# Two row tiles' latent queries and keys turned by VectorE blocks and transfers, in another order of work

## The chip, the cores and the metric

The kernel runs on one core of a Trainium2 chip. The metric is the device time of one execution in microseconds. The kernel before takes 1025.74 us, the median of three runs (1025.30 to 1026.27).

## The reference

Two transformer blocks run one after the other on 256 rows (the sequence) of 1024 features in fp32: a first block (short convolution, gated feed-forward, sliding-window attention, feed-forward) and a second block, of which the middle concerns us. It projects the normalised rows with `w_in` into a latent part (256 + 128 + 32 features), the queries and keys of a retention layer (512 each), its values and its gates (512 each). The latent part is normalised and expanded by `w_uq` and `w_ukv` into 8 heads of queries, keys (64 plain + 32 rotated features) and values; softmax attention over all 256 rows follows. Retention (8 heads of 64) and the latent attention together go through `w_o`. Two feed-forward networks stand before and behind.

```python
def mla_group(c_q, c_kv, k_pe_raw, pos_f, q_norm, w_uq, kv_norm, w_ukv):
    q = (rms_norm(c_q, q_norm) @ w_uq).reshape(B, S, H, 64 + 32)
    q_nope, q_pe = q[..., :64], rope(q[..., 64:], pos_f)
    kv = (rms_norm(c_kv, kv_norm) @ w_ukv).reshape(B, S, H, 64 + 64)
    k_nope, v = kv[..., :64], kv[..., 64:]
    k_pe = rope(k_pe_raw[:, :, None, :], pos_f)[:, :, 0]
    ...
    s = einsum('bqhd,bkhd->bhqk', qn, k_nope) + einsum('bqhr,bkr->bhqk', qp, k_pe)
    p = softmax(s * MLA_SCALE, axis=-1)
    return einsum('bhqk,bkhd->bqhd', p, v)

def second_block(x, ...):
    h = x + 0.5 * swiglu_2(rms_norm(x, ffn1_norm), ...)
    proj = rms_norm(h, mix_norm) @ w_in
    c_q, c_kv, k_pe, r_q, r_k, r_v, r_g = split(proj, [256, 384, 416, 928, 1440, 1952])
    a = mla_group(c_q, c_kv, k_pe, ...)
    r = retention_group(r_q, r_k, r_v, r_g, ...)
    h = h + concatenate([a, r], axis=-1) @ w_o
    h = h + 0.5 * swiglu_2(rms_norm(h, ffn2_norm), ...)
    return rms_norm(h, final_norm)
```

## The kernel before

The 256 rows are two row tiles (t = 0 and 1) of 128. All weights stream from HBM in chunks of 128 x 1024 fp32 (512 KB), in one order fixed by tables of chunk numbers (`C_X`, `C_U`, `C_WO`) and, on the host side, by `weight_chunks`. SyncE loads chunk n into one of four raw buffers once chunk n - 4 has been split (`load_behind`). ScalarE makes `w_high` of a raw chunk, and VectorE `w_low`, the rest; twelve split chunks have room (`RING`), and chunk n + 12 may be split when TensorE has used chunk n for both row tiles. A product of one row tile with a chunk is three passes of two matmuls each: high by high, low rows by high, high by low weights. The first product with a chunk (t = 0) waits for its `w_high` before the first pass and for its `w_low` before the third (`chunk_passes` with `split`).

The order of work is written out by hand. `walk_latent` calls `step(name, ...)` in one sequence, every engine walks the same sequence, and each carries out in order the steps that it has a function for; semaphores tie them together. So an engine's own instructions keep the order of that list. The names of the stage:

- `X(i, t, c)`: chunk c of projection i for row tile t (i = 0 latent, 1 and 2 the retention queries and keys, 3 values, 4 gates). ScalarE copies each finished projection from PSUM (`copied`); the next one of that row tile waits for this copy (`x_out`).
- `R` (`refill`), `high`, `low`: the split of one more chunk on ScalarE and VectorE, and on SyncE the load four chunks further.
- `LAT(t)`: the latent rows are normalised and turned by three TensorE transposes. `U(t)`: the expanding product with three chunks (18 matmuls), whose results ScalarE copies as `mq` (queries), `mk` (keys), `mv` (values), and VectorE's rotation of the 32 position features of `mq`. `KPE(t)`: the rotation of the shared key part, copied into `mk`.
- `MT(t)`: 16 TensorE transposes of 128x96 turn `mq` and `mk` by heads into PSUM; ScalarE copies the queries to `mqT`, VectorE the keys to `mkT`.
- `MS(v)`: round v = 0 to 7 computes the scores of two heads (two matmuls). `MS(v)` waits from v = 2 for the exponentials of round v - 2 (`mp_ready`), whose bank it overwrites. VectorE takes the maxima, `ME(v)` the exponentials on ScalarE, `MN(v)` the division on VectorE, `MPT(v)` four TensorE transposes of the probabilities with a ScalarE copy, `MPV(v)` the product with the values. Beside each round stands one product of projection 3 or 4.
- `RROPE`, `RB(t, part)`, `RV(t)`: rotation of the retention queries or keys, VectorE's transpose within 32x32 blocks, and the eight SBUF transfers (SyncE) that bring the blocks into place in `rT`. `RS(i)`, `RM`, `RPV`: the retention's products. `VC`: centring of its values, the last part of it on GpSimd. `decay`: its tables, made by ScalarE and GpSimd. `gate`, `MAT`, `SQ`, `VAR`, `GNvar`, `GNout`, `GT`, `RY`, `RL`, `Oc(t, kt)`: the rest of the layer and its output product.

Ahead of the stage come FFN3 and its join, behind it FFN4, neither of which the change touches.

## Time and profile before

| | |
|---|---|
| median of 3 runs | 1025.74 us (1025.30 to 1026.27) |
| profiled execution | 1026.88 us, of which the span of the trace is 1025.1 us |
| PE busy | 1015.6 us (99%), 4764 matmuls |
| VectorE, ScalarE busy | 686.6 us (67%), 564.4 us (55%) |
| GpSimd busy | 140.7 us (14%) |
| chain that ended last | PE 93%, DVE 3% |
| DMA | 204.61 MB, mean 200 GB/s |
| granted TensorE clock | 0.998 of full speed over the run |

The stage that is changed lies between about 722 and 830 us of the span. In the rows, a start is in us from the start of the span; PE is TensorE, DVE VectorE, ACT ScalarE, POOL GpSimd, SPq the queue that SyncE feeds. A bracket at a row's end is the idle time of that engine before it and what ended it. Matmuls overlap, so what a group of them costs is the distance from its start to the next group's start, not its busy time.

### The profile page before, as it was taken

What the parts mean: (1) busy time and instruction counts of PE and PEld (TensorE: products, weight loads), DVE (VectorE), ACT (ScalarE), POOL (GpSimd) and SP (SyncE); (2) the same over time, 40 slices, a digit from 0 to 9 for tenths busy, and PEclk for the clock granted to TensorE, in tenths of its full rate; (3) what the DMA queues carried; (4) which work ended last, traced back from release to release, by engine and by line L of the source; (5) the groups of instructions that cost most, each with busy time, mean ns of one, the idle gap of its engine ahead of it and who ended that gap; (6) DMA issues with size and microseconds to landing.
All of it is one profiled execution on the core that took longest, in us unless ns stands there. A gap on an engine that the chain in (4) does not pass through costs nothing.

```text
span 1025.1 us, 14271 instructions
## 1 busy us (share of the span) xinstructions
PE 1015.6 (99%) x4764; PEld 836.6 (82%) x4764; DVE 686.6 (67%) x1041; ACT 564.4 (55%) x923; POOL 140.7 (14%) x219
## 2 busy tenths in 40 slices
PE   9999999999999999999999999999999999999997
PEld 6999888888877778888888888888887688888886
DVE  6777865646688985656568565656788785655643
ACT  6665654545567764444556454454676854454542
POOL 1001450000143253000014000000400221000002
PEclk9999999999999999999999999999999999999999
DMA  9574567566643467657576665757653455756551
GB/s 369 187 243 168 195 222 240 183 221 206 207 144 125 145 226 251 224 195 239 180 232 195 231 214 191 244 175 243 200 184 124 146 184 182 245 184 231 195 168 46
DMA packets 109694, 204.61 MB, mean 200 GB/s; under 512 B 57472, under 2 KB 62992, under 8 KB 109648
## 3 DMA queue, kind: packets, MB, share of 16 engines
q1 hardware_dynamic: 107472, 198.55, 57.9%
q0 software_dynamic: 1888, 5.17, 1.6%
q8 instruction: 25, 0.41, 0.2%
q10 hardware_dynamic: 288, 0.31, 0.1%
q14 instruction: 21, 0.17, 0.0%
HBM read 187.20 MB, written 1.05 MB: 184 GB/s over the span
## 4 chain that ended last, share of the span: by engine, by line
PE 93%; DVE 3%; DMA 1%; ACT 1%; SPq 1%; POOL 0%; issue 0%; POOLq 0%; DVEq 0%; ACTq 0%
PE pG L2185 16%; PE pG L2177 16%; PE pG L2181 16%; PE pD L2177 11%; PE pD L2181 11%; PE pD L2185 11%; PE pG L2158 2%; PE pG L2160 1%; PE pG L2164 1%; PE pT L2194 1%; DVE w_low L1735 1%; DMA h<-in_x 1%; PE pD L2158 1%; PE pD L2164 1%; PE pD L2160 1%; PE pT L2379 1%
## 5 line engine op out<-in xcount | busy, mean ns | idle before, releaser
L1735 DVE TENSOR_TENSOR w_low<-raw,w_high 128x1024 fp32r<-128x1024 f32 x339 | 408.9, 1226 | 181.4 <-ACT w_high L1424 171.3
L1424 ACT ACTIVATE w_high<-raw 128x1024 fp32r<-128x1024 f32 x340 | 353.5, 1056 | 192.1 <-PE pG L2185 134.4
L2177 PE MATMUL pG<-w_high,xTh 128*128 128x512 f32 x712 | 219.8, 390 | 0.0
L2185 PE MATMUL pG<-w_low,xTh 128*128 128x512 f32 x712 | 219.4, 389 | 0.2 <-DVE w_low L1735 0.2
L2181 PE MATMUL pG<-w_high,xTl 128*128 128x512 f32 x712 | 219.3, 389 | 0.0
L2185 PEld LDWEIGHTS pG<-w_low,xTh 128*128 128x128 f32 x712 | 133.6, 188 | 28.3 <-DVE w_low L1735 0.6
L2181 PEld LDWEIGHTS pG<-w_high,xTl 128*128 128x128 f32 x712 | 133.5, 188 | 28.0 <-DVE xTl L1795 0.2
L2177 PEld LDWEIGHTS pG<-w_high,xTh 128*128 128x128 f32 x712 | 133.2, 188 | 27.5
L1531 ACT ACTIVATE gate<-pG,stat 128x256 f32<-128x256 f32 x102 | 48.4, 474 | 151.8 <-PE pG L2185 135.9
L2177 PE MATMUL pD<-w_high,aTh 128*128 128x512 f32 x348 | 107.8, 391 | 0.0
L2181 PE MATMUL pD<-w_high,aTl 128*128 128x512 f32 x348 | 107.4, 390 | 0.1
L2185 PE MATMUL pD<-w_low,aTh 128*128 128x512 f32 x348 | 107.4, 390 | 0.0
L1911 DVE SCALAR_TENSOR_TENSOR act<-pG,stat,gate 128x256 f32<-128x256 f32 x88 | 43.9, 499 | 84.3 <-ACT gate L1531 84.3
L2181 PEld LDWEIGHTS pD<-w_high,aTl 128*128 128x128 f32 x348 | 65.2, 188 | 14.3 <-DVE aTl L1939 0.8
L2185 PEld LDWEIGHTS pD<-w_low,aTh 128*128 128x128 f32 x348 | 65.2, 188 | 14.0 <-DVE w_low L1735 0.4
L2177 PEld LDWEIGHTS pD<-w_high,aTh 128*128 128x128 f32 x348 | 64.8, 188 | 12.2
L2177 PE MATMUL pD<-w_high,xTh 128*128 128x512 f32 (+1 forms) x144 | 47.6, 411 | 0.0
L1312 POOL TENSOR_SCALAR stat<-stat 128x1 f32<-128x1 f32 x8 | 2.8, 354 | 306.8 <-ACT junk L1513 306.6
L2181 PE MATMUL pD<-w_high,xTl 128*128 128x512 f32 (+1 forms) x144 | 44.3, 389 | 0.0
L2185 PE MATMUL pD<-w_low,xTh 128*128 128x512 f32 (+1 forms) x144 | 43.9, 386 | 0.0
L1319 POOL DMA_DIRECT2D xF<-hg x32 | 18.1, 571 | 172.6 <-DVE hg L1823 172.4
L1556 ACT ACTIVATE aTh<-aF 128x256 fp32r<-128x256 f32 x80 | 32.8, 410 | 13.4 <-DMA aF<-aB 13.4
(318 smaller groups left out, 1113.0 us busy)
## 6 DMA issues: line engine op xcount, KB each, us to landing
raw<-in_stream SPq DMA_DIRECT2D x340, 512.0 KB, 4.3
aF<-aB SPq DMA_DIRECT2D x320, 32.0 KB, 2.5
post<-in_posts POOLq DMA_DIRECT2D x5, 512.0 KB, 5.9
early<-in_stream SPq DMA_DIRECT2D x4, 512.0 KB, 12.5
xF<-hg SPq DMA_DIRECT2D x32, 64.0 KB, 2.5
xF<-hg POOLq DMA_DIRECT2D x32, 64.0 KB, 2.2
h<-in_x SPq DMA_DIRECT2D x2, 512.0 KB, 11.6
first_w<-in_opening SPq DMA_DIRECT2D x2, 384.0 KB, 4.2
```

The source lines that it names most:

```text
L1319: pool.dma_start(xF[t][:, first + 128 * a:first + 128 * a + 128], hg[t][32 * a:32 * a + 32, first:first + 512]).then_inc(hF_sent[half], 16)
L1424: sc.activation(w_high[:, slot(static):slot(static) + CHUNK], raw_of(static), ACT.Copy).then_inc(w_high_done, 1)
L1531: sc.activation(gate[t][:], gate_bank(ph, t, b)[:, 0:256], ACT.Copy if ph.mixer else ACT.Silu, scale=rr[t]).then_inc(gate_ready[t], 1)
L1556: sc.activation(act_parts(ph, t, b)[0][:].rearrange("p k (a r) -> p k a r", a=4), turned_act(ph, t, b), ACT.Copy).then_inc(ah_ready[t], 1)
L1735: ve.tensor_tensor(w_low[:, slot(static):slot(static) + CHUNK], raw_of(static), w_high[:, slot(static):slot(static) + CHUNK].bitcast(F32), ...
L1911: ve.scalar_tensor_tensor(dst, up, rr[t], by, ALU.mult, ALU.mult).then_inc(act_ready[t], 1)
L2158: pe.matmul(dst, ah, hi, start=start, stop=False)
L2160: pe.matmul(dst, ah, lo, start=False, stop=False)
L2164: return pe.matmul(dst, al, hi, start=False, stop=stop)
L2177: pe.matmul(dst, ah, w_high[:, where:where + n], start=start, stop=False)
L2181: pe.matmul(dst, al, w_high[:, where:where + n], start=False, stop=False)
L2185: mm = pe.matmul(dst, ah, w_low[:, where:where + n], start=False, stop=stop)
```

## The change

- `MT` is gone. `MB(t)` has VectorE transpose `mq` and `mk` (both now 128x768, laid out in blocks of 32 columns by a reordering of the weights on the host; `mk` repeats the shared part for each head) within 32x32 blocks. `MV(t)` moves the turned rows into `mqT` and `mkT` with eight SBUF transfers of 96 KB each, four issued by SyncE and four by GpSimd. The queries' transfers write runs of 128 B (768 of them each), the keys' runs of 1 KB. SyncE and GpSimd wait in order for the two transposes. The score matmuls read the same shapes as before through new strides.
- `RV(t)` is cut in two: SyncE moves the queries' four blocks, GpSimd the keys' four (512 runs of 128 B each). `RV(0)` stands right behind `MS(4)`, `RV(1)` behind `MS(7)`.
- `U(1)`, the second row tile's expanding product, stands ahead of the four chunks of `X(2, 1)` rather than behind them, and `KPE(1)` before it.
- The weight stream is reordered: the three chunks of `U` are now the 9th to 11th of the stage (`C_FIRST + 8`) and those of `X(2)` the 12th to 15th. `X(2, 0)` still runs before `U(0)` on TensorE.
- Refills stand elsewhere: of six splits between the copy of `X(1, 1)` and the copies of `U(1)` one is left, and five in a row stand behind them. In the rounds the order becomes scores, then the transposes of two rounds ago (`MPT(v - 2)`), then exponentials and division; chunk 24's split moves from round 1 to rounds 6 and 7, chunk 25's from round 3 to the end of the rounds. One more product (`X(3, 1, 0)`) stands before `MS(0)`, so one fewer stands within.

```diff
 C_FIRST = FFN3.first_chunk + FFN3.chunks
-C_X = [C_FIRST, C_FIRST + 4, C_FIRST + 8, C_FIRST + 15, C_FIRST + 19]
-C_U = C_FIRST + 12
+C_X = [C_FIRST, C_FIRST + 4, C_FIRST + 11, C_FIRST + 15, C_FIRST + 19]
+C_U = C_FIRST + 8
...
     step("U", 0)
     project(1, 1, 0)
     step("LAT", 1)
+    step("MB", 0)
+    step("MV", 0)
     for c in range(1, 4):
         project(1, 1, c)
+    refill(step, freed, 1)
+    step("KPE", 1)
+    step("U", 1)
+    freed += [C_U, C_U + 1, C_U + 2]
+    step("MB", 1)
+    step("MV", 1)
     refill(step, freed, 2)
-    step("MT", 0)
-    refill(step, freed, 2)
-    step("KPE", 1)
     for c in range(4):
         project(2, 1, c)
-        if c in (1, 2):
+        if c in (0, 1, 2):
             refill(step, freed, 1)
-    step("U", 1)
     step("exp_table",)
     step("RROPE", 1, 0)
     refill(step, freed, 1)
-    freed += [C_U, C_U + 1, C_U + 2]
     projects(3, 0, range(2))
-    step("MT", 1)
     refill(step, freed, 1)
     behind_maxima = freed.pop(0) + RING
     step("high", behind_maxima)
     projects(3, 0, range(2, 4))
+    step("RB", 0, 0)
+    project(3, 1, 0)
     step("MS", 0)
-    step("low", behind_maxima)
     step("ME", 0)
-    step("RB", 0, 0)
-    step("RB", 0, 1)
-    beside = [(3, 1, c) for c in range(4)] + [(4, 0, c) for c in range(4)] + [(4, 1, 0)]
-    project(*beside.pop(0))
-    project(*beside.pop(0))
+    project(3, 1, 1)
+    beside = [(3, 1, 2), (3, 1, 3)] + [(4, 0, c) for c in range(4)] + [(4, 1, 0)]
     for v in range(1, 8):
+        step("MS", v)
+        if v in (4, 7):
+            step("RV", v // 5)
+        if v >= 2:
+            step("MPT", v - 2)
+        step("ME", v)
         step("MN", v - 1)
-        step("MS", v)
-        if v in (1, 3):
-            refill(step, freed, 1)
-        step("ME", v)
+        if v == 1:
+            step("low", behind_maxima)
+        if v == 6:
+            behind_sums = freed.pop(0) + RING
+            step("high", behind_sums)
+        if v == 7:
+            step("low", behind_sums)
+        project(*beside.pop(0))
         if v in (3, 5, 7):
             step("MPV", v - 3)
             step("MPV", v - 2)
-        project(*beside.pop(0))
-        step("MPT", v - 1)
         if v == 2:
+            step("RB", 0, 1)
+        if v == 3:
+            step("RROPE", 1, 1)
+        if v == 4:
             step("VC", 0)
-        if v == 4:
-            step("RV", 0)
-            step("RROPE", 1, 1)
         if v == 5:
             step("RSUM",)
             step("RB", 1, 0)
         if v == 6:
             step("RB", 1, 1)
-        if v == 7:
-            step("RV", 1)
-            step("VC", 1)
         if v in (2, 4, 6):
             step("decay", v // 2 - 1)
     step("MN", 7)
-    refill(step, freed, 2)
+    step("VC", 1)
+    refill(step, freed, 3)
     project(4, 1, 1)
+    step("MPT", 6)
     step("MPT", 7)
     step("MAT", 0)
...
@@ MV on SyncE, RV on SyncE
 
+            def MV(t, ph):
+                sp.wait_ge(mB_ready, 2 * t + 1)
+                for a in range(0, 2):
+                    sp.dma_start(mqT[:, t, :, a, :], mq_turned[t][32 * a:32 * a + 32, :]).then_inc(m_moved, 16)
+                sp.wait_ge(mB_ready, 2 * t + 2)
+                for a in range(0, 2):
+                    sp.dma_start(mkT[:, t, a, :, :], mk_turned[t][32 * a:32 * a + 32, :]).then_inc(m_moved, 16)
+
             def RV(t, ph):
                 sp.wait_ge(ms_psum, 4 * (t + 1))
-                for part in range(2):
-                    sp.wait_ge(rB_ready, 2 * t + part + 1)
-                    for a in range(4):
-                        dst = rkT[:, t, :, a, :] if part else rqT[:, t, a, :, :]
-                        sp.dma_start(dst, block_turned(t, part)[32 * a:32 * a + 32, :]).then_inc(rT_moved[t], 16)
+                if t == 1:
+                    sp.wait_ge(rqT_moved, 64)
+                sp.wait_ge(rB_ready, 2 * t + 1)
+                for a in range(4):
+                    sp.dma_start(rqT[:, t, a, :, :], block_turned(t, 0)[32 * a:32 * a + 32, :]).then_inc(rqT_moved, 16)
...
@@ GpSimd
+            def MV(t, ph):
+                pool.wait_ge(mB_ready, 2 * t + 1)
+                for a in range(2, 4):
+                    pool.dma_start(mqT[:, t, :, a, :], mq_turned[t][32 * a:32 * a + 32, :]).then_inc(m_sent, 16)
+                pool.wait_ge(mB_ready, 2 * t + 2)
+                for a in range(2, 4):
+                    pool.dma_start(mkT[:, t, a, :, :], mk_turned[t][32 * a:32 * a + 32, :]).then_inc(m_sent, 16)
+
+            def RV(t, ph):
+                pool.wait_ge(ms_psum, 4 * (t + 1))
+                pool.wait_ge(rB_ready, 2 * t + 2)
+                for a in range(4):
+                    pool.dma_start(rkT[:, t, :, a, :], block_turned(t, 1)[32 * a:32 * a + 32, :]).then_inc(rkT_moved, 16)
...
@@ ScalarE
-                if c == 3 and i < 4 and (i, t) != (2, 1):
+                if c == 3 and i < 4:
                     copied(i, t)
...
+                if i == 3:
+                    sc.wait_ge(m_moved, 128)
+                    sc.wait_ge(m_sent, 128)
...
@@ VectorE
+            def MB(t, ph):
+
+                ve.wait_ge(mqk_ready, 2 * t + 2)
+                ve.transpose(mq_turned[t], mq[:]).then_inc(mB_ready, 1)
+                ve.wait_ge(u_out, 4 * t + 3)
+                ve.transpose(mk_turned[t], mk[:]).then_inc(mB_ready, 1)
...
@@ TensorE
-            def MT(t, ph):
-                pe.wait_ge(mqk_ready[t], 2)
...
+                    pe.wait_ge(m_moved, 128)
+                    pe.wait_ge(m_sent, 128)
+                    pe.wait_ge(u_out, 8)
```

The first place is TensorE between `LAT(1)` and the end of `X(2, 1)`; `lat`, `mq`, `mk` are the latent rows, queries and keys, `latTh` and `latTl` the turned latent rows, `xTh1` the second row tile. Before, from the last chunk of `X(1, 1)` on:

```order
L2177 MATMUL pD1<-w_high_50,xTh1_53 128x512 x2
L2181 MATMUL pD1<-w_high_50,xTl1_55 128x512 x2
L2185 MATMUL pD1<-w_low_51,xTh1_53 128x512 x2
L2194 MATMUL pG0<-consts_62,mq_131 96x128 x4
L2194 MATMUL pT0<-consts_62,mq_131 96x128 x4
L2194 MATMUL pG1<-consts_62,mk_132 96x128 x4
L2194 MATMUL pT1<-consts_62,mk_132 96x128 x4
L2177 MATMUL pD1<-w_high_50,xTh1_53 128x512 x2
L2181 MATMUL pD1<-w_high_50,xTl1_55 128x512 x2
```

And now:

```order
L2215 MATMUL pD1<-w_high_50,xTh1_53 128x512 x2
L2219 MATMUL pD1<-w_high_50,xTl1_55 128x512 x2
L2223 MATMUL pD1<-w_low_51,xTh1_53 128x512 x2
L2196 MATMUL pG0<-w_high_50,latTh_84 128x384
L2198 MATMUL pG0<-w_low_51,latTh_84 128x384
L2202 MATMUL pG0<-w_high_50,latTl_85 128x384
L2196 MATMUL pT0<-w_high_50,latTh_84 128x384
L2198 MATMUL pT0<-w_low_51,latTh_84 128x384
L2202 MATMUL pT0<-w_high_50,latTl_85 128x384
```

The four rows of transposes are gone, and the expanding product (the six rows with `latTh` or `latTl`, and twelve more) follows at once, where the first chunk of `X(2, 1)` stood.

The second place is ScalarE from the copy of `X(1, 1)` to the exponentials of round 0; `w_high<-raw` is the split of one chunk, `rqk<-pD1` and `rv0<-pD0` copies of projections, `mp0,lsum0` the exponentials. Before, from `X(1, 1)`'s copy to that of `X(2, 1)`:

```order
L1618 ACTIVATE rqk_138<-pD1,stat_64 128x512
L1424 ACTIVATE w_high_50<-raw_49 128x1024 x2
L1651 ACTIVATE mqT_126<-pG0 96x512
L1651 ACTIVATE mqT_126<-pT0 96x512
L1424 ACTIVATE w_high_50<-raw_49 128x1024 x4
L1638 ACTIVATE mq_131<-pG0,stat_64 128x384
L1638 ACTIVATE mq_131<-pT0,stat_64 128x384
L1642 ACTIVATE mk_132<-pG1,stat_64 128x8x64
L1644 ACTIVATE mv1_134<-pT1,stat_64 128x512
L1618 ACTIVATE rqk_138<-pD1,stat_64 128x512
```

And now, to the exponentials:

```order
L1657 ACTIVATE rqk_140<-pD1,stat_65 128x512
L1460 ACTIVATE w_high_50<-raw_49 128x1024
L1677 ACTIVATE mq_132<-pG0,stat_65 128x384
L1677 ACTIVATE mq_132<-pT0,stat_65 128x384
L1681 ACTIVATE mk_133<-pG1,stat_65 128x512
L1683 ACTIVATE mv1_136<-pT1,stat_65 128x512
L1460 ACTIVATE w_high_50<-raw_49 128x1024 x5
L1657 ACTIVATE rqk_140<-pD1,stat_65 128x512
L1476 ACT_TABLE_LOAD
L1460 ACTIVATE w_high_50<-raw_49 128x1024 x3
L1657 ACTIVATE rv0_141<-pD0,stat_65 128x512
L1694 ACTIVATE mp0_145,lsum0_73<-pG0,negm0_71 128x256 x2
```

The copies of the expanded queries, keys and values moved up past five splits; five splits then stand in a row ahead of the copy of `X(2, 1)`, and three ahead of the copy of `X(3, 0)` and of the exponentials.

The third place is TensorE in rounds 1 and 2; `mp0` holds probabilities, `mkT,mqT` marks scores. Before:

```order
L2496 MATMUL pG1<-mkT_128,mqT_126 128x256 x2
L2177 MATMUL pD1<-w_high_50,xTh1_53 128x512 x2
L2181 MATMUL pD1<-w_high_50,xTl1_55 128x512 x2
L2185 MATMUL pD1<-w_low_51,xTh1_53 128x512 x2
L2194 MATMUL pT0<-consts_62,mp0_141 128x128 x4
L2496 MATMUL pG0<-mkT_128,mqT_126 128x256 x2
L2177 MATMUL pD1<-w_high_50,xTh1_53 128x512 x2
```

And now:

```order
L2524 MATMUL pG1<-mkT_129,mqT_127 128x256 x2
L2215 MATMUL pD1<-w_high_50,xTh1_53 128x512 x2
L2219 MATMUL pD1<-w_high_50,xTl1_55 128x512 x2
L2223 MATMUL pD1<-w_low_51,xTh1_53 128x512 x2
L2524 MATMUL pG0<-mkT_129,mqT_127 128x256 x2
L2232 MATMUL pT0<-consts_63,mp0_145 128x128 x4
L2215 MATMUL pD1<-w_high_50,xTh1_53 128x512 x2
```

The scores of round 2 now stand before the transposes of round 0's probabilities, not behind them.

## Rows read from the trace of the kernel before

**Rows 1.** The page's first part: busy time and share of the span of each engine.

```profile
PE 1015.6 (99%) x4764; PEld 836.6 (82%) x4764; DVE 686.6 (67%) x1041; ACT 564.4 (55%) x923; POOL 140.7 (14%) x219
```

**Rows 2.** Waits of PE over the span: us in total, times, longest.

```profile
PE pG L2530 <- DMA rT<-rqk: 1.0, 1, 1.0
PE pD L2515 <- ACT mpT L1670: 0.3, 1, 0.3
```

**Rows 3.** Timeline of PE, 737 to 754 us: start, duration, line, operation.

```profile
737.44 0.63 PE L2177 MATMUL pD<-w_high,xTh 128*128 128x512 f32 x2
...
742.93 0.33 PE L2158 MATMUL pG<-w_high,latTh 128*128 128x384 f32 x1
...
746.43 0.62 PE L2177 MATMUL pD<-w_high,xTh 128*128 128x512 f32 x2
...
747.80 0.49 PE L2194 MATMUL pD<-consts,lat 128*128 128x128 f32 x3
...
752.25 0.60 PE L2194 MATMUL pG<-consts,mq 128*96 128x128 f32 x4
...
753.91 0.70 PE L2177 MATMUL pD<-w_high,xTh 128*128 128x512 f32 x2
```

**Rows 4.** Timeline of PE, 770 to 803 us.

```profile
770.22 1.03 PE L2496 MATMUL pG<-mkT,mqT 96*128 96x256 f32 x4
...
773.83 1.03 PE L2496 MATMUL pG<-mkT,mqT 96*128 96x256 f32 x4
...
776.08 0.60 PE L2194 MATMUL pT<-consts,mp 128*128 128x128 f32 x4
...
792.93 1.03 PE L2496 MATMUL pG<-mkT,mqT 96*128 96x256 f32 x4
...
802.29 1.14 PE L2530 MATMUL pG<-rT 64*128 64x256 f32 x8 [1.03 <-DMA rT<-rqk]
```

**Rows 5.** Timeline of ACT, 739 to 743 us.

```profile
739.15 2.23 ACT L1424 ACTIVATE w_high<-raw 128x1024 fp32r<-128x1024 f32 x2
...
742.44 1.06 ACT L1424 ACTIVATE w_high<-raw 128x1024 fp32r<-128x1024 f32 x1 [0.56 <-DMA raw<-in_stream]
```

**Rows 6.** Timeline of DVE, 740 to 774 us.

```profile
740.23 2.41 DVE L1735 TENSOR_TENSOR w_low<-raw,w_high 128x1024 fp32r<-128x1024 f32 x2 [0.39 <-ACT w_high L1424]
...
759.86 0.16 DVE L2034 TENSOR_TENSOR mpT<-lat,trig 128x16 f32<-128x16 f32 x1
...
760.82 2.35 DVE L1735 TENSOR_TENSOR w_low<-raw,w_high 128x1024 fp32r<-128x1024 f32 x2
763.09 0.28 DVE L2034 TENSOR_TENSOR mpT<-mq,trig 128x128 f32<-128x128 f32 x1
...
764.43 0.42 DVE L2034 TENSOR_TENSOR ttmp<-rqk,trig 128x256 f32<-128x256 f32 x1
...
773.22 1.30 DVE L2021 STREAM_TRANSPOSE post<-rqk 128x512 f32<-128x512 f32 x2
```

**Rows 7.** Timeline of SyncE's queue, 755 to 756 us.

```profile
755.37 0.33 SPq L1158 DMA_DIRECT2D raw<-in_stream  x1
```

**Rows 8.** Timeline of ACT, 758 to 773 us.

```profile
758.46 1.06 ACT L1424 ACTIVATE w_high<-raw 128x1024 fp32r<-128x1024 f32 x1 [0.57 <-DMA raw<-in_stream]
760.68 1.06 ACT L1424 ACTIVATE w_high<-raw 128x1024 fp32r<-128x1024 f32 x1 [1.16 <-DMA raw<-in_stream]
...
770.42 0.69 ACT L1618 ACTIVATE rv<-pD,stat 128x512 f32<-128x512 f32 x1 [0.17 <-PE pD L2185]
772.22 0.47 ACT L1663 ACTIVATE mp<-pG,negm 128x256 f32<-128x256 f32 x1 [1.11 <-DVE negm L2083]
```

**Rows 9.** The transfers into rT: issue in ns min/median/max, and landing.

```profile
L1190 SPq DMA_DIRECT2D rT<-post x8: 549/632/646, 784.7 to 789.3; - x8
...
DMA to landing us min/median/max: 2.1/2.4/3.6
```

**Rows 10.** GpSimd's issues of the like: ns min/median/max.

```profile
L1319 POOL DMA_DIRECT2D xF<-hg x32: 534/554/648, 276.7 to 842.3; - x32
```

94 lines of the change are left out of this document (43 added, 51 removed).

## The prediction

> **What bounds the kernel now.** I read the page's first part for who is busy, then TensorE's waits, then the timelines of TensorE, ScalarE and VectorE through the stage, SyncE's queue, and last the rows on transfers. TensorE works 1015.6 of 1025.1 us [rows 1], and all it waits for in this stage is 1.03 us for a transfer into `rT` and 0.30 us for one copy of probabilities [rows 2]. So what leaves TensorE shortens the kernel one for one, and a delay elsewhere costs nothing until TensorE meets it. Whether it does is the question: in the stage ScalarE and VectorE already wait for raw weights and for one another [rows 5, 6, 8].
>
> **What TensorE loses and gains in work.** Two `MT` steps go. The first takes from 752.25 to 753.91, 1.66 us [rows 3]; the next product's first pair is drawn out by about 0.1 (0.70 busy instead of 0.62). That is 1.76 each, 3.52 for two. The `rT` wait (1.03) should go: before, one queue issues the eight last transfers, 0.63 each [rows 9], the last landing up to 3.6 after its issue; now two queues issue four each. From the start of `MS(7)` to the point where `RS(0)` was ready was 802.29 - 1.03 - 792.93 = 8.33 us [rows 4], and with `MPT(5)` added behind `MS(7)` (0.44) it is 8.8. `RV(1)` may start once the scores are done, 0.7 after `MS(7)` starts, so it has 8.0 us; four issues and a landing need 4 x 0.63 + 3.6 = 6.1. The 0.30 wait goes too. Credits: 3.52 + 1.03 + 0.30 = 4.85 us. The order within a round costs TensorE nothing more: the same matmuls, one pair of neighbours exchanged; 0 to 0.3 us in all for other overlaps, taken as 0.
>
> **The weight order, first debit.** `X(2, 0)` starts at 737.44 and takes 5.49 to 742.93, 1.37 a chunk [rows 3]. Before, it read the stage's 9th to 12th chunks; now the 12th to 15th (numbers 11 to 14 from 0). Nothing ahead of it changes, so the splits come when they came. Number 11 is ready. Number 12 is the first of the two `w_high` from 739.15; each takes 1.06, and its `w_low` begins at 740.23, which marks the high part as done; TensorE wanted it at 738.83. It starts at 740.23, two passes to 741.15, then waits for `w_low` at 740.23 + 1.23 = 741.46, and ends at 741.92. Number 13 (`w_low` done by 742.64) fits: 743.29. Number 14's `w_high` starts only at 742.44, when its raw chunk has landed, and is done at 743.50; `w_low` 1.23 later, 744.75; the third pass from there ends at 745.24 [rows 5, 6]. `U(0)` starts then, not at 742.93: a loss of 2.31 us. The three chunks of `U`, split sooner, gain nothing, as they were not waited for. This term is the surest of all, because both engines walk up to it unchanged.
>
> **The middle, no debit on TensorE.** `U(0)` 3.50 (742.93 to 746.43), one chunk 1.37 and `LAT(1)` with three chunks 4.45 (747.80 to 752.25) [rows 3] put the end of `X(1, 1)` at 754.56. `U(1)` follows to 758.06 (its latent rows are ready before, as VectorE and ScalarE reach `LAT(1)` as before). Then `X(2, 1)` to 763.55, `X(3, 0)` to 769.03, `X(3, 1, 0)` to 770.40, then `MS(0)`. Here I am 1.2 us ahead in work, 3.52 - 2.31.
>
> **The chain behind `U(1)`, second debit.** ScalarE copies `X(1, 1)` from 754.76 (a copy is 0.69 busy, 0.6 to the next one's start [rows 8]) and makes one `w_high` until 756.4; VectorE's `w_low` takes 1.23 to 757.6; `KPE(1)` 0.96 (759.86 to 760.82 before); the rotation 1.34 (763.09 to 764.43); two block transposes: two of 512 columns take 1.30, so two of 768 are estimated at 1.94 [rows 6]. So `MB(1)` ends at 761.8. Only behind it stands the `w_low` of chunk 16, done at 763.0, and this is what SyncE waits for to load chunk 20, after its four `MV(1)` issues (also done by 763.1). Before, chunk 19's load was issued at 755.37 [rows 7] and ended ScalarE's wait at 758.46; the next, one `w_low` behind it, ended another at 760.68 [rows 8]: a lone load lands 3.1 us after its issue and the next 2.2 behind. So raw 20 lands at 766.2, 21 at 768.4, 22 at 770.6, 23 at 772.8. ScalarE must do the `w_high` of 21, 22, 23 in order before `copied(3, 0)` and `ME(0)`: 772.8 + 1.06 + 0.6 = 774.5, exponentials 0.9 (two of 0.47), 775.4. VectorE arrives at about the same time: `w_low` 20, the retention rotation, `w_low` 21 and 22, a transpose and the maxima stand in a row and end near 774.7. Before, `ME(0)` started at 772.22, 2.0 behind `MS(0)`; now 4.1. `MS(2)` comes 4.5 after `MS(0)` (two scores with a chunk each, 2.25 apart: 773.83 to 776.08 [rows 4]), at 774.9, and waits for those exponentials: 0.5 us. `MV(1)` moves 768 KB beside load 20, more than a chunk's 512 KB, so that load may be up to 0.9 later: wait 0.5 to 1.4, and I take 0.9. `X(3, 1, 0)` needs the copy behind `w_high` 20, about 768.0 to 768.9 against 769.03: just in time.
>
> **Third debit, the rounds.** `MPT(1)` waits for a division that stands behind `w_low` 23 and round 2's maxima: about 0.3. `MPV(1)` waits for a copy behind a table's three ScalarE operations: 0.2. From round 4 on VectorE has fewer splits than before and keeps up, and so does ScalarE: each pair of rounds holds one `MPV` pair. The three splits at the end of the rounds end 1 us before the copies of `MPT(6)` and `MPT(7)` are due. Bounds of this part 0 to 1.2, taken as 0.5. `MV(0)` and `MV(1)` cost SyncE eight issues of 0.63 and GpSimd eight; what is queued behind SyncE's is chunk 19's load (needed by ScalarE after 762) and chunk 20's, counted above. Nothing waits on GpSimd behind `MV` before round 3. `m_moved` and `m_sent` are full by about 766 against `MS(0)` at 770.4.
>
> **Sum.** 4.85 - 2.31 - 0.9 - 0.5 = 1.14 us gained. The profiled execution, 1026.88 with a span of 1025.10, would become 1025.74 with a span of 1023.96. The three runs' median is 1.14 below the profiled one, 1025.74, so it becomes 1024.6. The rest of the kernel is bound by TensorE and keeps the lead.
>
> **GpSimd's transfers.** GpSimd issues 32 transfers of 64 KB in 0.534 to 0.648 us each, many beside VectorE operations [rows 10]; all write runs of 512 B. What one with 768 or 512 runs of 128 B costs it, the trace doesn't show. From the like on SyncE (549 to 646 ns, half of them with runs of 128 B and half with 512 B [rows 9]) it is nothing more; by the number of runs (6 and 4 times the 128 of rows 10) it is 3.3 and 2.2 us. I take 0.6. The Trainium skill, SBUF — State Buffer (SBUF: two separate sides), says that a DMA issued from GpSimd starves while VectorE holds the port pair the two share, about 3.1 us instead of 0.62. Rows 10 with their maximum of 0.648 don't show it. By its figure, an estimate from that page, four issues of 12.4 us would make `RS(0)` wait some 7 us.
>
> **Rivals.**
> - *GpSimd's issues grow with the runs* (slower). `RV(1)`'s keys: 4 x 2.2 + 2.4 landing = 11.2 us where 8.0 are free, so `RS(0)` waits 3.2; `MV(1)`: two of 3.3, two of 0.6 and a landing end at 771, 0.6 after `MS(0)`. Together 3.8 on top, 2.7 slower than before: 1028.4. It decides from (8.0 - 2.4)/4 = 1.4 us an issue. For it: one engine makes these issues and none like them is in the trace. Against: rows 9, where runs cost no issue time.
> - *The lead passes through.* The waits in the rounds don't appear, since loads land as closely as they are issued, 1.2 apart instead of 2.2, and ScalarE catches up. Gain 4.85 - 2.31 = 2.54: 1023.2. Against it: the four loads can't be issued before their `w_low`.
> - *The rounds take all back.* ScalarE and VectorE start the rounds 2 us behind and the wait repeats at `MS(3)` and `MPT(2)`, 1 us more: 1025.7, no change.
>
> **Chances.** Forecast 0.52, its own range 1023.7 to 1025.5. All given back 0.20. Passes through 0.15. GpSimd slow 0.13. A measurement of this kernel tells 0.2%, 2.05 us, from no change: faster than 1023.69 gets the pass-through and a little of the forecast's edge, 0.17; slower than 1027.79 most of the GpSimd case, 0.11; the rest, 0.72, is within. The range runs from 1023.1 to 1027.6: it takes in the pass-through's value and smaller issue costs on GpSimd and leaves the full GpSimd case out.
>
> **What the new profile should show.** TensorE waits 1.4 for a `w_high` and 0.3 for a `w_low` in the second chunk of `X(2, 0)`, and 0.2 and 0.3 in the fourth, `U(0)` starting near 745.2. No 128x96 transposes; `U(1)` near 754.6; `MS(0)` near 770.4; `MS(2)` waiting about 0.9 for ScalarE; `RS(0)` near 801 with no transfer waited for. VectorE's 128x768 transposes take about 1.0. It is wrong if `X(2, 0)` isn't held up (then over 3 us faster), if GpSimd's issues exceed 1.4 us, or if `MS(0)` waits for the transfers.

## The result and the profile after

Over 12 runs each on the same chips the changed kernel takes 1029.67 us (1027.32 to 1030.32), the kernel before 1026.07 (1025.3 to 1027.37): a ratio of 1.0031, 95% interval 1.0023 to 1.0039, so 3.6 us slower by the medians, 3.2 by the ratio, where 1.1 faster was forecast. The prediction was wrong in size and sign, and its range (to 1027.6) missed the time. The profiled execution of the changed kernel took 1027.74 with a span of 1025.9. That is near its fastest; a second profile (e1_again, below) shows the usual one.

TensorE has 32 instructions fewer than in [rows 1] and is busy for 2.0 us less; GpSimd has 16 more, the transfers:

```profile
PE 1013.6 (99%) x4732; PEld 832.9 (81%) x4732; DVE 687.4 (67%) x1041; ACT 563.4 (55%) x919; POOL 153.2 (15%) x235
```

TensorE's waits between 700 and 850 us (us in total, times, longest), where [rows 2] had 1.0 for `rT` and 0.3 for `mpT`:

```profile
PE pG L2524 <- ACT mp L1694: 1.4, 1, 1.4
PE pD L2215 <- ACT rqk L1657: 1.4, 1, 1.4
PE pD L2215 <- ACT w_high L1460: 0.7, 1, 0.7
```

The timeline of TensorE at the points of [rows 3, 4]: start, duration, operation, in brackets the idle time ahead of it and what ended it.

```profile
737.53 0.63 PE L2215 MATMUL pD<-w_high,xTh 128*128 128x512 f32 x2
...
739.78 0.73 PE L2215 MATMUL pD<-w_high,xTh 128*128 128x512 f32 x2 [0.70 <-ACT w_high L1460]
...
744.50 0.33 PE L2196 MATMUL pG<-w_high,latTh 128*128 128x384 f32 x1
...
753.79 0.33 PE L2196 MATMUL pG<-w_high,latTh 128*128 128x384 f32 x1
...
769.71 0.73 PE L2215 MATMUL pD<-w_high,xTh 128*128 128x512 f32 x2 [1.37 <-ACT rqk L1657]
...
771.20 1.03 PE L2524 MATMUL pG<-mkT,mqT 96*128 96x256 f32 x4
...
777.26 1.13 PE L2524 MATMUL pG<-mkT,mqT 96*128 96x256 f32 x4 [1.39 <-ACT mp L1694]
...
802.08 1.13 PE L2558 MATMUL pG<-rT 64*128 64x256 f32 x8
```

The reader is to see four things. `X(2, 0)` waits 0.70 in its second chunk and `U(0)` starts at 744.50. `U(1)` starts at 753.79, sooner by the missing `MT(0)`. Then two waits of 1.4 stand before `X(3, 1, 0)` and `MS(2)`, and `RS(0)` comes only 0.2 sooner than before.

Both waits go back to one transfer. These are ScalarE (first fence) and SyncE's queue (second):

```profile
758.64 4.08 ACT L1460 ACTIVATE w_high<-raw 128x1024 fp32r<-128x1024 f32 x4
768.02 1.06 ACT L1460 ACTIVATE w_high<-raw 128x1024 fp32r<-128x1024 f32 x1 [5.30 <-DMA raw<-in_stream]
768.99 0.67 ACT L1657 ACTIVATE rqk<-pD,stat 128x512 f32<-128x512 f32 x1
769.68 1.28 ACT L1476 ACT_TABLE_LOAD   x1
770.97 2.96 ACT L1460 ACTIVATE w_high<-raw 128x1024 fp32r<-128x1024 f32 x3
773.83 0.67 ACT L1657 ACTIVATE rv<-pD,stat 128x512 f32<-128x512 f32 x1
776.18 0.47 ACT L1694 ACTIVATE mp<-pG,negm 128x256 f32<-128x256 f32 x1 [1.68 <-DVE negm L2121]
```

```profile
760.24 1.30 SPq L1201 DMA_DIRECT2D mqT<-mq_turned  x2
761.59 1.34 SPq L1204 DMA_DIRECT2D mkT<-mk_turned  x2
762.97 7.73 SPq L1172 DMA_DIRECT2D raw<-in_stream  x5
```

Load 20 (of the chunk with that number, the stage's first being 0) is issued at 762.97, behind the four `MV(1)` transfers of SyncE and beside GpSimd's. It lands 5.0 us later, at 768.0, not 3.1 later. ScalarE stands still for 5.30 us in front of it, and behind it in ScalarE's row are the copy of `X(2, 1)`, for which `X(3, 1, 0)` waits, and everything up to `ME(0)`, for which `MS(2)` waits. VectorE waits for the same high part; its `w_low` 20, a rotation, two more splits, a transpose and the maxima end at 776. Chunks 21 to 23 were there when ScalarE came to them: in this execution not four loads but one set the time.

What the DMA engines did meanwhile (stretch, its length, busy time and instructions of TensorE, granted clock, share of the DMA engines, GB/s):

```profile
762.00:764.00 2.00, 2.00 (x10) 1.00 0.99 193
764.00:766.00 2.00, 2.00 (x11) 1.00 0.91 254
766.00:768.00 2.00, 2.00 (x11) 1.00 0.96 357
768.00:770.00 2.00, 0.63 (x3) 1.00 1.02 408
```

With the `MV` transfers under way the engines are as busy (0.91 to 0.99) at 193 to 254 GB/s as later at 357 to 408 with loads alone. In SyncE's queue between 750 and 770 us a packet of 128 B (queries) takes 12 ns on average, one of 1024 B (keys) 56 and one of 4096 B (loads) 176: 11, 18 and 23 bytes a ns. The Trainium skill, DMA: Bandwidth & Descriptors (Specifications), asks for pieces of at least 512 B for full rate; the queries of `MV` go in runs of 128 B, and the trace agrees with the direction of that rule. The Trainium skill exempts transfers within SBUF from the penalty of small pieces (the same page, Why small descriptors are slow); `MV`'s are such transfers, and this trace doesn't agree with that.

The packets also show where load 20 was. It is issued at 762.97, but its first packet moves at 764.96, when SyncE's `MV(1)` packets, which are in the same queue, are nearly through (the last ends at 765.93). In the kernel before, load 19, with nothing ahead of it, is issued at 755.37 and its first packet moves at 756.33. So 1.0 us of the lateness is a wait in SyncE's own queue, and the rest comes after the first packet.

### The profile page after: what moved, and what is told of

It reads as the page before. It is cut to its first block, busy times and chain, and to the rows that moved or that the text cites. A ratio compares the mean times of both kernels' runs of the same rounds, so it can differ in the third digit from the quotient of the medians.

```text
span 1025.9 us, 14224 instructions
## 1 busy us (share of the span) xinstructions
PE 1013.6 (99%) x4732; PEld 832.9 (81%) x4732; DVE 687.4 (67%) x1041; ACT 563.4 (55%) x919; POOL 153.2 (15%) x235
## 4 chain that ended last, share of the span: by engine, by line
PE 89%; DVE 5%; DMA 2%; ACT 2%; issue 1%; POOL 0%; SPq 0%; POOLq 0%; DVEq 0%; ACTq 0%
PE pG L2223 16%; PE pG L2215 16%; PE pG L2219 16%; PE pD L2215 10%; PE pD L2219 10%; PE pD L2223 10%; DVE w_low L1768 2%; PE pG L2196 2%; PE pG L2202 1%; PE pG L2198 1%; PE pT L2232 1%; DMA raw<-in_stream 1%; DMA h<-in_x 1%; ACT w_high L1460 1%; PE pD L2202 1%
```

## The experiments

Ratios are to the kernel before, run in between on the same chip, with the 95% interval. "The end" is the span less the start of TensorE's last matmul.

**e1_again: the changed kernel, unedited.**

> The changed kernel once more, nothing edited, for a second profiled execution. Its runs spread over 3 us (1027.3 to 1030.3) and the profiled one was near the low end, so the trace that is there may miss what costs the usual run 2 us more. Theory 1 (the chain behind U(1)): an execution above 1029 shows TensorE's waits before X(3, 1, 0) and MS(2), 1.4 us each in the first trace, grown to 2 to 3 us each, with raw chunks 20 to 23 landing later. Rival 2 (the weight order): the wait in X(2, 0), 0.7 before, grows to 2 or more. Rival 3 (the rounds): new waits between MS(3) and RS(0), or for rT. Ratio to the kernel before 1.0025 to 1.004 by all.

Measured: 1028.82 us, 1.0028 [1.0016, 1.0040]; the profiled execution 1029.12, span 1027.3. Waits of TensorE, then ScalarE, then the same columns as above by microsecond:

```profile
PE pD L2215 <- ACT rqk L1657: 2.6, 1, 2.6
PE pD L2215 <- ACT w_high L1460: 0.7, 1, 0.7
```

```profile
769.48 1.06 ACT L1460 ACTIVATE w_high<-raw 128x1024 fp32r<-128x1024 f32 x1 [6.63 <-DMA raw<-in_stream]
```

```profile
769.00:770.00 1.00, 0.00 (x0) 1.00 1.01 389
770.00:771.00 1.00, 0.00 (x0) 0.92 0.98 401
771.00:772.00 1.00, 0.84 (x2) 0.50 0.31 123
772.00:773.00 1.00, 1.00 (x3) 0.50 0.41 74
773.00:774.00 1.00, 1.00 (x4) 0.50 0.83 270
774.00:775.00 1.00, 1.00 (x6) 0.88 0.50 201
```

Load 20 was issued at 763.18 and landed 6.3 us later. The wait before `X(3, 1, 0)` grew from 1.37 to 2.62, and near its end TensorE's granted clock fell from 1.0 (2.4 GHz) to 0.5 (1.2 GHz) and stayed there until 774.2: three matmuls a microsecond instead of six, about 1.5 us of work lost. In exchange `MS(2)` didn't wait in this one, where theory 1 had both waits grow. So theory 1 holds for the first wait, with a price that it didn't have. The rivals' waits are not there: `X(2, 0)` waits 0.7 as before, `rT` nothing. The Trainium skill, TensorE: Matmul & The Clock Gate (What's actually happening), says that idleness halves this clock; here it did so in one wait of 2.62 us and in none of 1.4.

**e2_u0first: U(0) ahead of X(2, 0).**

```
-    projects(2, 0)
-    step("RROPE", 0, 1)
     step("KPE", 0)
     step("U", 0)
+    projects(2, 0)
+    step("RROPE", 0, 1)
```

> The changed kernel with KPE(0) and U(0) moved ahead of X(2, 0), so that the weights are read in the order in which they are split. Theory 1: X(2, 0) no longer waits for w_high 12 and w_low 12 to 14 (1.5 us on TensorE in the first trace), and everything up to the end of X(1, 1) comes 1.5 earlier, but MS(0) and MS(2) hang on loads 20 to 23, which hang on VectorE's row behind MB(1), also up to 1.5 earlier; so half to all of 1.5 us comes back: 1.0 to 1.5 us faster than the changed kernel, still slower than the kernel before. Rival 2: the weight order is the cause of the whole loss, and this runs at or below the kernel before (3 us and more faster than the changed one). Rival 3: the same as theory 1 with 1.5.

Measured: 1028.65, 1.0031 [1.0019, 1.0043]. No gain at all. `U(0)` now waits 1.73 for `latT`, the price of what it saves; and the waits behind are as in the changed kernel, 1.5 and 1.4. So this run doesn't separate the theories as it was meant to: it swaps one debit for another of about the same size. That the weight order is not the whole loss follows from the two waits behind it, not from this run's time.

**e3_oldrounds: the order of rounds as before.**

```
-    step("RB", 0, 0)
-    project(3, 1, 0)
     step("MS", 0)
+    step("low", behind_maxima)
     step("ME", 0)
...
+        step("MPT", v - 1)
```

> The changed kernel with the walk from X(3, 0) to MPT(7) as in the kernel before: RB(0, 0), RB(0, 1) and two products between MS(0) and MS(1), MPT(v - 1) at the end of round v, w_low 23 before ME(0), splits 24 and 25 in rounds 1 and 3. The transfers stay on two queues. Theory 1: MS(0) no longer needs copied(3, 0) and X(3, 1, 0) ahead of it, and MS(1) has two chunks of cover, so the waits before X(3, 1, 0) and MS(2) shrink from 2.8 us to under 1.5; 1 to 2 us faster than the changed kernel. Rival 2: no difference within 0.5 us. Rival 3 (the order of rounds is what costs): 3 us faster, at the time of the kernel before or below.

Measured: 1032.03, 1.0064 [1.0050, 1.0077]: 3 us slower than the changed kernel, against all three theories.

```profile
PE pT L2226 <- DVE mp L2122: 3.7, 1, 3.7
PE pD L2209 <- ACT rqk L1651: 2.1, 1, 2.1
PE pD L2209 <- ACT w_high L1454: 1.1, 2, 0.7
```

Load 20 landed 6.7 us after its issue. With the old order the transposes of `MPT(0)` come before `MS(2)` and need the whole row of ScalarE and VectorE up to the division: 3.73 us, and the clock was at 0.5 from 781.1 to 787.9 (this profiled execution took 1034.61, 2.6 above the run's median). The new order of rounds is no cause of the loss; with late loads it protects.

**e4_b_u1early: the kernel before with the weight order alone.**

```
-C_X = [C_FIRST, C_FIRST + 4, C_FIRST + 8, C_FIRST + 15, C_FIRST + 19]
-C_U = C_FIRST + 12
+C_X = [C_FIRST, C_FIRST + 4, C_FIRST + 11, C_FIRST + 15, C_FIRST + 19]
+C_U = C_FIRST + 8
...
     step("KPE", 1)
+    step("U", 1)
+    freed += [C_U, C_U + 1, C_U + 2]
     for c in range(4):
         project(2, 1, c)
```

> The kernel before with one part of the change alone: weights in the stream order X0, X1, U, X2 and so U(1) ahead of X(2, 1); the turning of mq and mk stays on TensorE (MT(0) and MT(1)). Theory 1: X(2, 0) is held up by 1.5 us as in the changed kernel; nothing else moves much, since MT(1) now has all of X(2, 1) as cover: 1.0 to 2.0 us slower than the kernel before. Rival 2 (the weight order is the whole loss): 3 to 4 us slower. Rival 3: 1.5 us slower as theory 1.

Measured: 1033.4, 1.0073 [1.0060, 1.0087]: 7.5 us, about twice the most that any of the three expected. The `X(2, 0)` part is as in the changed kernel (0.7 for `w_high`, `U(0)` at 744.50). The rest is a wait of 3.7 before `U(1)` for the copies of `MT(0)` and a clock of 0.5 from 759.2 to 762.6. The order of weights calls for `U(1)` early, and with `MT` on TensorE that is dear: the two parts of the change belong together.

**e5_copy_first: the split of chunk 20 behind the table load.**

```
-        if c in (0, 1, 2):
+        if c in (0, 1):
             refill(step, freed, 1)
     step("exp_table",)
     step("RROPE", 1, 0)
-    refill(step, freed, 1)
+    refill(step, freed, 2)
```

> The changed kernel with the split of chunk 20 moved from inside X(2, 1) to behind RROPE(1, 0), so that on ScalarE copied(2, 1) and the table load stand ahead of w_high 20, which waits 5.3 to 6.6 us for its raw chunk. Theory 1 (raw 20 lands late, and everything in ScalarE's row stands behind it): the wait before X(3, 1, 0), 1.4 to 2.6, is gone, and with it the fall of the clock that followed it; but w_high 20 to 23 and VectorE's w_low 20 to 22 still start at 768 to 769.5, so ME(0) comes at the same time and MS(2) waits longer by what was gained before it, 2.8 in all: 0.5 to 1.5 us faster than the changed kernel, by the table load that is now early (1.3 us) and by the clock. Rival (the copy's place alone is the fault): 2.5 to 3.5 us faster, at the time of the kernel before.

Measured: 1029.11, 1.0029 [1.0018, 1.0040]. The wait before `X(3, 1, 0)` is gone, and the one at `MS(2)` is 2.33 instead, with the clock at 0.5 from 777.6 to 781, so the gain of 0.5 to 1.5 us that was expected isn't there. The row, not the copy's place in it, is what counts.

**e6_split16_early, e7_both, e8_load_before_mv, e9_both_loads_first: loads ahead of MV(1).** e6 moves the split of chunk 16 ahead of `KPE(1)`:

```
-    refill(step, freed, 1)
+    refill(step, freed, 2)
     step("KPE", 1)
     step("U", 1)
     freed += [C_U, C_U + 1, C_U + 2]
     step("MB", 1)
     step("MV", 1)
-    refill(step, freed, 2)
+    refill(step, freed, 1)
```

> The changed kernel with the split of chunk 16 moved ahead of KPE(1), U(1) and MB(1) (two splits there instead of one, and one instead of two behind MV(1)). Load 20 is then issued near 758 instead of 763 and ahead of the MV(1) transfers. Theory 1: raw 20 is there when ScalarE comes to it near 763; no wait before X(3, 1, 0), no fall of the clock; w_low 17 to 20 end one after the other from 764 on, and the wait at MS(2) shrinks or goes: 2.5 to 4 us faster than the changed kernel, so at or up to 1 us below the kernel before. Price: MB(1) and MV(1) 1.2 us later, landing near 768 against MS(0) near 769.8. Rival (the transfers of MV(1) slow down any load beside them, whatever its place): load 21 takes 20's place, and under 1.5 us come back.

e7 puts `KPE(0)` and `U(0)` behind the first chunk of `X(2, 0)` besides:

```
-    projects(2, 0)
+    project(2, 0, 0)
+    step("KPE", 0)
+    step("U", 0)
+    for c in range(1, 4):
+        project(2, 0, c)
```

> The kernel e6_split16_early with, besides, KPE(0) and U(0) put between the first and the second chunk of X(2, 0), so that the weights' order costs less there. Theory 1: once nothing downstream hangs on load 20, the 1.2 to 1.5 us that X(2, 0) loses count on their own: the wait for w_high 12 (0.7) and the small ones for w_low go, a wait of about 0.3 for latT comes (in e2_u0first U(0) could start at 738.8, here it is reached at 738.9): 0.8 to 1.4 us faster than e6_split16_early. Rival (the loads set the pace anyway, as in e2_u0first, where 1.5 us gained at X(2, 0) were lost again): no difference within 0.3 us.

e8 is the changed kernel with `MV(1)` behind two splits (shown), e9 is e7 with `MV(1)` behind its one:

```
-    step("MV", 1)
     refill(step, freed, 2)
+    step("MV", 1)
```

> The changed kernel with step MV(1) behind the splits of chunks 16 and 17 in the walk: on SyncE loads 20 and 21 are issued ahead of its four MV(1) transfers; VectorE's and ScalarE's order doesn't change, and GpSimd's four transfers go as before. Theory 1 with a collision: load 20 is issued at 762.3 instead of 763.0 and has only half of MV(1) beside it; it lands 1 to 2 us sooner, the wait before X(3, 1, 0) falls to under 0.7, and the clock stays up; SyncE's part of MV(1) is issued from 764 to 766.5 and lands near 770, so MS(0) may wait up to 1 us: 0.5 to 2 us faster than the changed kernel. Rival (the load is slow by itself, its 5 to 6 us have nothing to do with MV(1)): 0.7 us sooner by its issue alone, and what MS(0) then waits makes it no faster or slower.

> The kernel e7_both with step MV(1) behind the split of chunk 17, so that loads 20 and 21 both stand ahead of SyncE's half of MV(1). In e7_both load 21 stood behind it, ended a ScalarE wait of 2.6 us, and MS(2) waited 1.6. Theory 1 (a load issued behind MV(1) lands 5 to 7 us after its issue, one ahead of it 3.5 to 4): load 21 lands 1.5 to 2 us sooner, ME(0) too, MS(2) waits under 0.7: 0.5 to 1.2 us faster than e7_both. Rival (the row of splits on VectorE sets ME(0), not the load): no difference within 0.3 us.

Measured: e6 1027.24, 1.0014 [1.0005, 1.0023]; e7 1025.99, 1.0000 [0.9991, 1.0009]; e8 1027.69, 1.0020 [1.0011, 1.0029]; e9 1025.45, 0.9998 [0.9989, 1.0007]. ScalarE's wait for load 20 in e8, where only the order on SyncE differs from the changed kernel:

```profile
765.88 1.06 ACT L1460 ACTIVATE w_high<-raw 128x1024 fp32r<-128x1024 f32 x1 [3.92 <-DMA raw<-in_stream]
```

It was issued at 761.62 and landed 4.2 us later, its first packet moving 1.0 after the issue, and TensorE no longer waits before `X(3, 1, 0)`. This profile is of the fastest of e8's 11 executions (1025.81 against a median of 1027.69). By the ratios e8 gains 0.8 to 1.1 us on the changed kernel, and the intervals overlap. In e6 it is load 21 that stands behind `MV(1)`; it was issued at 764.75 and landed at 771.68, 6.9 later, and `MS(2)` waited 2.9. That is the expected rival in part, but this profile is of e6's slowest execution (1031.16, median 1027.24). In e9 none of the first two is, and what stays is this:

```profile
PE pG L2526 <- ACT mp L1696: 1.1, 1, 1.1
PE pG L2526 <- DMA mkT<-mk_turned: 0.6, 1, 0.6
PE pG L2198 <- DVE latTl L2032: 0.4, 1, 0.4
```

e7 against e6 gives 1.3 us for the cure of `X(2, 0)`, as theory 1 had it: once load 20 doesn't bind, that debit counts on its own. e9 against e7 gives only 0.2 by the ratios, where 0.5 to 1.2 was expected, so its rival (the row of splits sets `ME(0)`, not the load) isn't ruled out.

Where a load stands is not all, as the landings of other loads show. In the kernel before, a load with nothing ahead of it landed 3.1 to 3.4 us after its issue, and one right behind another load 4.2 to 5.1 (its two profiles). In e9 loads 19 and 20 are issued at 755.91 and 756.60, right behind `MV(0)`, and land 6.8 and 7.5 us later; that is as late as load 20 or later, but it costs little, since they are issued 6 us sooner than load 20 of the changed kernel. And load 22 of e9, issued at 765.45 right behind SyncE's half of `MV(1)`, lands 4.4 later; GpSimd's half had been issued by 762.8. So what is dear seems to be a load issued while both halves are under way, and what e6, e7 and e9 gain is in good part the sooner issue.

**e12_mv_more: the opposite, three transfers more in MV(1)** (`m_first` and `m_sent0` count those of `MV(0)`).

```
             def MV(t, ph):
                 pool.wait_ge(mB_ready, 2 * t + 1)
+                if t == 1:
+                    pool.wait_ge(m_first, 64)
+                    pool.wait_ge(m_sent0, 64)
+                    for a in range(3):
+                        pool.dma_start(spare[:, a, :, :], mq_turned[1][32 * a:32 * a + 32, :]).then_inc(m_sent if t else m_sent0, 16)
```

> The changed kernel with three more transfers of 96 KB in GpSimd's MV(1), ahead of its own, from mq_turned into unused memory; SyncE's queue and the issue of load 20 (763.0) don't change. Theory 1 with a collision: the bytes in small runs ahead of and beside load 20 grow from 768 to 1056 KB; load 20 lands 1 to 2 us later than 5.0 to 6.3 after its issue, the wait before X(3, 1, 0) passes 2.6 in most executions, the clock falls in most, and the transfers themselves land near 770: 2 to 4 us slower than the changed kernel. Rival (load 20 is late for another reason): it lands 5 to 6.3 us after its issue as before, and only the last transfers, near 770, may hold up MS(0): 0 to 1 us slower.

Measured: 1030.52, 1.0050 [1.0036, 1.0064], about 2 us slower than the changed kernel by the ratios. In the profile load 20, issued at 763.58, landed at 769.63, 6.05 later; the wait before `X(3, 1, 0)` is 2.33, `MS(0)` waits 0.5 for `mkT`, and the clock stayed at 1.0 in this one. The time and the longer wait agree with the collision; 6.05 lies inside the 5.0 to 6.3 of the changed kernel, so load 20's own lateness is not shown to have grown. That of the next three has: loads 21 to 23 land 8.5 to 9.1 us after their issue, against 5.9 to 7.4 in the two profiles of the changed kernel.

**e10_best, e13_splits_late, e14_decay_late: what is left.** e10 is e9 with `w_high` 23 behind `ME(1)` and `decay(2)` in round 7; e13 is e9 with the splits of chunks 22 and 23 in rounds 1 and 3 and `RB(0, 0)` behind `ME(0)`; e14 adds `decay(2)` in round 7 to that.

```
-    step("high", behind_maxima)
...
+            step("high", behind_maxima)
             step("low", behind_maxima)
...
-        if v in (2, 4, 6):
+        if v in (2, 4):
             step("decay", v // 2 - 1)
+        if v == 7:
+            step("decay", 2)
```

And in e13 and e14 (parts):

```
+    projects(3, 0)
     project(3, 1, 0)
     step("MS", 0)
     step("ME", 0)
+    step("RB", 0, 0)
...
+        if v in (1, 3):
+            refill(step, freed, 1)
```

> The kernel e9_both_loads_first with two small moves: w_high of the chunk behind the maxima stands behind ME(1) and not ahead of the copy of X(3, 0), so that ME(0) doesn't wait for that chunk's load; and decay(2) stands in round 7 and not in round 6, so that GpSimd's RV(1) isn't held by a decay multiplication (in the changed kernel its issues began 2.0 us behind SyncE's, and in e7_both the last landing cost TensorE 0.9). Theory 1: MS(2)'s wait falls by up to 1.2 more and no rT wait is left: 1 to 2 us faster than e9_both_loads_first, 1 to 2.5 us faster than the kernel before. Rival (other orders on the full engines just move the wait on): within 0.5 us of e9_both_loads_first, a wait for w_high or dm in place of those.

> The kernel e9_both_loads_first with the splits of chunks 22 and 23 in rounds 1 and 3, as the kernel before has two there, and RB(0, 0) behind ME(0). On VectorE w_low 22 and the transpose no longer stand between X(3, 0) and the first maxima, and ScalarE has no w_high 22 and 23 ahead of the copy of X(3, 0) and ME(0). Theory 1 (the row of splits, held by the loads, sets ME(0)): ME(0) starts 1.5 to 2.5 us sooner than 773.6, the wait at MS(2), 1.1, goes; what stays is 0.4 for latT and 0.6 for the landing of mkT; the rounds hold one more split pair in round 3: 0.7 to 1.3 us faster than e9_both_loads_first, 1 to 2 us faster than the kernel before. Rival (every place for a split costs the same, since VectorE's row is full up to round 3): the wait moves to MS(3) or MPT(1), within 0.3 us.

> The kernel e13_splits_late with decay(2) in round 7 instead of round 6, so that on GpSimd RV(1) doesn't stand behind a decay multiplication. Theory: where TensorE reaches RS(0) before the last key transfer, up to 0.9 us (seen in e7_both), none in e9_both_loads_first: 0 to 0.9 us faster than e13_splits_late. Rival: nothing is waited for there, no difference.

Measured: e10 1025.89, 1.0001 [0.9991, 1.0010]; e13 1027.06, 1.0010 [1.0001, 1.0019]; e14 1026.52, 1.0009 [1.0000, 1.0018]. In e10 `MS(2)` still waits 1.2 and `MPT(1)` 0.9. In e13 the wait at `MS(2)` is gone, but transposes wait twice for VectorE's division, 2.5 in all, and `MS(0)` waits 1.5 for `mkT`. The rivals held, in e13 with more against it than they said: it is over 1 us slower than e9, where no change was their value. The two engines' rows are full, and a wait moved out of one place stands in the next.

**e11_b_two_queues and e15_before_again: the credit for rT.** e11 is the kernel before with `RV`'s keys on GpSimd; e15 is the kernel before, unedited.

```
+            def RV(t, ph):
+                pool.wait_ge(ms_psum, 4 * (t + 1))
+                pool.wait_ge(rB_ready, 2 * t + 2)
+                for a in range(4):
+                    pool.dma_start(rkT[:, t, :, a, :], block_turned(t, 1)[32 * a:32 * a + 32, :]).then_inc(rkT_moved, 16)
```

> The kernel before with one part of the change alone: RV's transfers of keys on GpSimd, those of queries on SyncE. Theory 1: of the 1.03 us that TensorE waited for rT, 1.9 us of SyncE's issues go (four of 0.63, less the start of GpSimd's behind its decay multiplication), so the wait goes wholly: 0.8 to 1.1 us faster than the kernel before. Rival (GpSimd's small-run transfers land as late, up to 4.1 us in the changed kernel): within 0.3 us.

> The kernel before once more, nothing edited, for a second profiled execution. Its first one had a wait of 1.03 us for rT and took 1026.88, 0.8 to 1.1 above its medians; e11_b_two_queues, which has no such wait, is no faster than those medians. Theory: in the usual execution the rT wait is under 0.3 us, so this credit of the prediction was mostly not there to be had. Rival: the wait is 0.8 to 1.1 in this one too, and the two queues lose as much elsewhere.

Measured: e11 1025.57, 0.9998 [0.9989, 1.0007]; e15 one run, 1025.62 with a span of 1023.8, right at the medians. Its `RS(0)`:

```profile
801.00 1.13 PE L2530 MATMUL pG<-rT 64*128 64x256 f32 x8
```

No wait stands in front, where [rows 4] had 1.03. The landings of its `rT` transfers were 2.1 to 2.8 us, against up to 3.6 in [rows 9]. e4, with all of `RV` on SyncE as before, has no such wait either. So the wait was a matter of the one execution first profiled, and two queues for `RV` are worth nothing; in e7, with two queues, `RS(0)` even waited 0.9 for `rT`.

**e16_all_synce and e17_rv_synce: the end of the span.** e16 is e9 with all `MV` and `RV` transfers on SyncE, e17 is e9 with those of `RV` alone on SyncE:

```
             def RV(t, ph):
                 sp.wait_ge(ms_psum, 4 * (t + 1))
...
+                sp.wait_ge(rB_ready, 2 * t + 2)
+                for a in range(4):
+                    sp.dma_start(rkT[:, t, :, a, :], block_turned(t, 1)[32 * a:32 * a + 32, :]).then_inc(rkT_moved, 16)
```

> The kernel e9_both_loads_first with no transfer of MV or RV on GpSimd: SyncE issues them all, the queries (MQ) and keys (MK) of a row tile as two steps, MK(0) behind loads 19 and 20, load 21 between MQ(1) and MK(1), RV as in the kernel before. What it tells: in the profiles the time from TensorE's last matmul to the end of the span is 6.62 to 6.65 us where GpSimd has none of these transfers, 6.82 with eight of RV (e11_b_two_queues), 7.45 to 7.51 with eight of MV besides, 7.72 with eleven of MV (e12_mv_more). Theory: the added end hangs on what GpSimd issued, so it is 6.65 here, and that alone makes it 0.8 us faster than e9_both_loads_first; the last landing before MS(0) stays at 768.5 to 769.5, so at most 0.5 us of it is lost again: 0.3 to 0.8 us faster than e9_both_loads_first. Rival (the end hangs on something else of the changed kernel, its code or its buffers): 7.5 again and no gain.

> The kernel e9_both_loads_first with RV's transfers alone back on SyncE, as in the kernel before (MV stays on two queues). Theory: the end of the span is 7.3 us behind the last matmul (7.5 less the 0.2 that e11_b_two_queues added to the kernel before), and RS(0) waits at most 0.3 for rT, as in e15_before_again: the same time as e9_both_loads_first within 0.3 us, so the second queue for RV was worth nothing. Rival: the wait for rT is 1 us, and the two queues are worth that.

Measured: e16 1027.3, 1.0011 [1.0002, 1.0020] (one of its 11 runs took 2067.66 us, and nothing that was recorded shows why; the median of the others is 1027.2); e17 1024.79, 0.9991 [0.9982, 1.0000]. e16 has the short end, 6.52 us, as expected, but SyncE's longer row made `mkT` land later: `MS(0)` waited 2.8 and the clock fell. e17 has an end of 6.85 and no wait for `rT`; its waits are 1.3 at `MS(2)` and 0.4 for `latT`. Both expectations missed in size: e16 is 1.3 us slower than e9 by the ratios instead of 0.3 to 0.8 faster, since its short end was paid for in `MS(0)`'s wait, and e17 is 0.7 faster instead of the same, with an end 0.45 shorter than foreseen. e17 is the fastest version here, 0.8 us below the kernel before and 4 below the changed one, and the first is at the edge of what can be told.

The page's row on GpSimd's queue (packets, MB, share) for e15, e11, e17, the changed kernel and e12, each from its own page:

```profile
q0 software_dynamic: 1888, 5.17, 1.8%
```

```profile
q0 software_dynamic: 2144, 5.69, 1.9%
```

```profile
q0 software_dynamic: 2272, 5.95, 2.0%
```

```profile
q0 software_dynamic: 2528, 6.48, 2.2%
```

```profile
q0 software_dynamic: 2672, 6.77, 2.2%
```

The ends that go with them are 6.62, 6.82, 6.85, 7.46 and 7.72 us. The last matmul of e15 and of the changed kernel, with spans of 1023.8 and 1025.9:

```profile
1017.18 0.28 PE L2164 MATMUL pT<-w_high,aTl 128*128 128x256 f32 x1
```

```profile
1018.44 0.28 PE L2202 MATMUL pT<-w_high,aTl 128*128 128x256 f32 x1
```

The output's transfers are issued at the same distance from the last matmul and land 2.0 to 2.7 us later in both kernels, so the 0.84 us lies behind them. In all 19 profiles the end follows what GpSimd issued, over 200 us after it did: 6.52 to 6.65 with 1888 packets, 7.45 to 7.51 with 2528. What the program waits for there the records don't show.

## Why the prediction was wrong

The usual execution of the changed kernel (e1_again, 1029.12) against the usual one of the kernel before (e15, 1025.62): 3.5 us, just what the medians say. It splits so, with starts of `X(2, 0)` 737.19 and 737.25, `U(0)` 744.70 and 742.74, `RS(0)` 803.59 and 801.00:

| part | before | changed | difference | predicted |
|---|---|---|---|---|
| up to `X(2, 0)` | 737.25 | 737.19 | -0.06 | 0 |
| `X(2, 0)` | 5.49 | 7.51 | +2.02 | +2.31 |
| `U(0)` to `RS(0)` | 58.26 | 58.89 | +0.63 | -2.42 |
| `RS(0)` to the last matmul | 216.18 | 216.26 | +0.08 | 0 |
| the end | 6.62 | 7.45 | +0.83 | 0 |

(The -2.42 is 3.52 and 0.30 less 0.9 and 0.5.) Without the 1.03 for `rT`, which was predicted on top, the forecast was thus no change, -0.11; measured were +3.5. Step by step:

- **MT's credit, 3.52: right.** `U(1)` starts 9.29 behind `U(0)`, where before, at 9.32, `MT(0)` stood [rows 3]. From `U(0)` to `MS(0)` are 26.70 us, 25.33 without the wait; predicted were 25.2. Of the credit that is 3.3: before, the same stretch took 27.29 with one product of 1.37 less in it.
- **The credit for rT, 1.03: wrong, and it could be seen.** It came from one execution, which lay 1.14 above the median shown; a wait of 1.03 in it was the likeliest reason. The prediction subtracted the 1.14 to reach the median and the 1.03 as well, so it counted the same microsecond twice. e15 and e11 show that it wasn't there.
- **X(2, 0), 2.31: right in mechanism, 0.3 to 0.8 too large.** 7.51 and 6.97 in the two profiles instead of 5.49. Number 14's raw chunk came in time, so the fourth chunk hardly waited (`U(0)` at 744.50 and 744.70, predicted 745.24).
- **The chain behind U(1), 0.9: this step failed.** The issue of load 20 (predicted 763.1, was 763.0) and the end of `MB(1)` (761.8, was 761.1) were right. The landing was taken from a load that had nothing ahead of it: 3.1 us. Load 20 behind `MV(1)` took 5.0 and 6.3 in the two profiles of the changed kernel, up to 6.7 in e3; 1.0 us of that is the time that it stood in SyncE's queue behind `MV(1)`'s packets. The spacing of 2.2 between loads was wrong the other way: loads 21 to 23 landed at 769.48, 770.74 and 771.97, 1.2 to 1.5 apart. The 0.9 that was added for the collision went to the last of four loads, while the first was late and the rest came close behind it. "Just in time" for `X(3, 1, 0)` had no margin, so the full lateness showed there and at `MS(2)`: 1.37 and 1.39 in one execution, 2.62 and none in the other. Against the 0.9 of the sum TensorE thus lost 2.76, or 2.62 and the clock's 1.5.
- **The clock was no term of the sum.** A wait that grew by 1.25 us cost 1.5 more on top, since TensorE then ran at 1.2 GHz until 774.2; 1.4 of the two came back at `MS(2)`, which no longer waited. This likely also makes the spread of 3 us: the landing of load 20 differs by 1.3 us between the two profiles. Two profiles don't show it.
- **The rounds, 0.5: right in size** (0.38 is what the 57.58 us from `U(0)` to `RS(0)` leave in the first profile; the two waits named for it aren't in the list, so where it went isn't shown), and e3 shows that the new order helps.
- **The end, 0.83: not thought of.** No row of the kernel before pointed to it.
- **The rivals.** GpSimd's issues took 0.75 to 0.89 us for 512 and 768 runs, so the slower rival fell by its own mechanism, and its 1.4 us was not reached; the page of the Trainium skill weighed there, SBUF — State Buffer, with its 3.1 us, is borne out by none of the 19 profiles, in which the longest transfer issue of GpSimd took 0.89. Slower had 0.11, all of it hung on this one mechanism; the lateness of load 20, bounded by 0.5 to 1.4, should have been bounded by the bytes ahead of it as well.

What is shown: that load 20 behind `MV(1)` binds (e6, e7 and e9 issue it 4 to 6 us sooner, and the wait before `X(3, 1, 0)` goes; e6 brings back half of the loss, and e7 and e9, with `X(2, 0)` cured too, all of it), that `rT`'s credit wasn't there, and that the end follows GpSimd's transfers. Less sure is what the place on SyncE's queue alone is worth (e8). Open is why, after its first packet has moved, a load behind `MV(1)` takes 3.0 us to land in one execution and 4.1 in the other, and what the end consists of.

## What to carry to other kernels

A landing time belongs to a load and to what is queued and under way beside it; a load that is issued behind transfers in small runs is not the same load, and the cure that worked here is to issue it some us sooner. Where a copy is "just in time", price the miss in full, and reckon with the clock: the waits here behind which it fell cost, by an estimate from their lengths and half the time at 0.5 that followed, 1.4 (e4) to 2.1 (e6, e16) times their length. And before a wait in a single profiled execution is counted as a credit, look whether that execution is slower than the median by as much.

## What the runs showed of the hardware

- The granted clock fell to 0.5 in or behind waits of 2.33 (e5), 2.62 (e1), 2.77 (e16), 2.89 (e6), 3.66 (e4) and 3.73 us (e3), for some 3 to 7 us; not behind 2.33 (e12), 2.14 (e3) or any shorter one. So the same wait can cost the clock or not.
- GpSimd's issue of a transfer with 768 runs of 128 B took 0.78 to 0.89 us, with 512 runs 0.75 to 0.84, and of `mkT`, whose runs are 1 KB at the far side, 0.56 to 0.58; SyncE's of the same kinds 0.54 to 0.70 in both kernels, but up to 0.95 where loads stand close ahead of `MV(1)` (e8, e9 and those built on e9) and once 1.59 in e16.
- Transfers that GpSimd issues go with a longer end of the program: 0.2 us for eight of `RV` or of `MV` alone, 0.83 for both, 1.1 with three more. So it isn't the same amount for each transfer, and the cause is not known.
